# Sixteen packs of memory's keys and values, placed one step of the pairs of heads earlier

## What is computed

```python
def memory_attention(h, mem_n, w_mq, w_mkv, w_mo):
    Bn, S, D = h.shape
    q = (h @ w_mq).reshape(Bn, S, MEM_HEADS, MEM_HEAD_DIM)
    k, v = jnp.split(mem_n @ w_mkv, 2, axis=-1)
...
    s = jnp.einsum('bqhd,bkhd->bhqk', q, k).astype(jnp.float32) * (MEM_HEAD_DIM ** -0.5)
    p = jax.nn.softmax(s, axis=-1)
    o = jnp.einsum('bhqk,bkhd->bqhd', p, v.astype(jnp.float32)).astype(h.dtype).reshape(Bn, S, D)
    return o @ w_mo
```

## Time and profile before

| | us |
|---|---|
| median of 3 runs | 2766.68 (2765.08 to 2767.01) |
| the profiled execution's own time | 2767.14 |
| its span in the trace | 2765.1 |
| PE busy | 2732.9 (99%) |
| DVE busy | 1168.9 (42%) |
| ACT busy | 1033.6 (37%) |
| POOL busy | 1110.3 (40%) |
| mean granted clock | 0.998 |

### The profile page before, as it was taken

How to read it: one execution, slowest core, us unless ns; L and a number is a source line. 1 busy time by engine, 2 the same in 40 slices (tenths; PEclk the granted TensorE clock), 3 DMA queues, 4 the chain that set the end, 5 groups by cost and what they waited for, 6 DMA issues and landing times.

```text
span 2765.1 us, 35465 instructions
## 1 busy us (share of the span) xinstructions
PE 2732.9 (99%) x12412; PEld 2171.7 (79%) x12412; DVE 1168.9 (42%) x1908; ACT 1033.6 (37%) x1584; POOL 1110.3 (40%) x473
## 2 busy tenths in 40 slices
PE   9999999999999999999999999999999999999998
PEld 7777777888888888857888888888888754888887
DVE  5886534655534224256883222122221366422212
ACT  4555534444333223343233222232222466422221
POOL 3234433444444443523224444544445410444443
PEclk9999999999999999999999999999999999999999
DMA  5333322333333332322113323333333210333332
GB/s 168 121 98 116 99 84 63 92 94 103 96 109 97 94 97 93 114 76 88 54 46 107 99 91 106 105 93 99 98 99 107 84 39 10 105 94 101 94 106 84
DMA packets 80029, 257.29 MB, mean 93 GB/s; under 512 B 11576, under 2 KB 16696, under 8 KB 79690
## 3 DMA queue, kind: packets, MB, share of 16 engines
q1 hardware_dynamic: 73712, 245.00, 28.9%
q10 hardware_dynamic: 6234, 11.17, 1.2%
HBM read 249.98 MB, written 6.03 MB: 93 GB/s over the span
## 4 chain that ended last, share of the span: by engine, by line
PE 89%; issue 6%; POOL 2%; DVE 2%; ACT 1%; DMA 0%; POOLq 0%; SPq 0%; DVEq 0%; ACTq 0%
PE ps L813 25%; PE ps L815 25%; PE ps L814 25%; POOL wlo L766 2%; PE ps L1453 1%; PE ps L1435 1%; PE ps L1422 1%; PE ps L1203 1%; PE ps L1232 1%; PE ps L1426 1%; PE ps L1182 1%; PE ps L1109 1%; PE ps L1251 1%; PE ps L1119 1%; PE ps L1042 0%
## 5 line engine op out<-in xcount | busy, mean ns | idle before, releaser
L766 POOL TENSOR_TENSOR wlo<-raw,whi 128x1024 fp32r<-128x1024 f32 x449 | 1098.0, 2449 | 1607.5 <-ACT whi L1522 1582.8
L813 PE MATMUL ps<-lin_hi,whi 128*128 128x512 f32 x2200 | 864.0, 393 | 0.0
L815 PE MATMUL ps<-lin_hi,wlo 128*128 128x512 f32 x2200 | 856.3, 389 | 0.0
L814 PE MATMUL ps<-lin_lo,whi 128*128 128x512 f32 x2200 | 856.1, 389 | 0.0
L1522 ACT ACTIVATE whi<-raw 128x1024 fp32r<-128x1024 f32 x452 | 473.1, 1052 | 524.0 <-PE ps L815 452.1
L813 PEld LDWEIGHTS ps<-lin_hi,whi 128*128 128x128 f32 x2200 | 413.0, 188 | 91.7 <-issue 5.5
L814 PEld LDWEIGHTS ps<-lin_lo,whi 128*128 128x128 f32 x2200 | 413.0, 188 | 88.1 <-issue 3.1
L815 PEld LDWEIGHTS ps<-lin_hi,wlo 128*128 128x128 f32 x2200 | 412.9, 188 | 86.6
L813 PE MATMUL ps<-act_hi,whi 128*128 128x512 f32 x858 | 334.0, 389 | 0.0
L815 PE MATMUL ps<-act_hi,wlo 128*128 128x512 f32 x858 | 333.8, 389 | 0.0
L814 PE MATMUL ps<-act_lo,whi 128*128 128x512 f32 x858 | 333.8, 389 | 0.0
(11 more groups left out here) (406 smaller groups left out, 2762.6 us busy)
## 6 DMA issues: line engine op xcount, KB each, us to landing
raw<-in_packs SPq DMA_DIRECT2D x456, 512.0 KB, 3.6
table<-bias_scratch ACTq DMA_DIRECT2D x12, 256.0 KB, 3.5
bias_scratch<-biasrow ACTq DMA_DIRECT2D x16, 160.0 KB
x<-in_x_t SPq DMA_DIRECT2D x4, 512.0 KB, 8.3
out_t<-x SPq DMA_DIRECT2D x16, 128.0 KB, 1.8
bias_scratch<-biasrow ACTq DMA_DIRECT2D x4, 320.0 KB
mem<-in_mem_t ACTq DMA_DIRECT2D x1, 1024.0 KB, 6.9
pool_count<-in_pool_count ACTq DMA_DIRECT2D x1, 1024.0 KB, 6.2
```

The costliest lines, as they stand in the source:

```text
L766: pool.tensor_tensor(wlo[:, n % 4, :], raw[:, n % 2, :], whi[:, n % 4, :].bitcast(F32), ALU.subtract).then_inc(low_split, 1)
L813: pe.matmul(target, wh, hi[:, k, :], start=(chunk0 + at == 0), stop=False)
L814: pe.matmul(target, wh, lo[:, k, :], start=False, stop=False)
L815: mm = pe.matmul(target, wl, hi[:, k, :], start=False, stop=(chunk0 + at == total - 1))
```

## The change

`KV_FROM` goes from 2 to 1. Memory pack p is now issued in step p + 1 instead of p + 2 on PE, and DVE takes its product out of the bank in step p + 1. Step 1 gets pack 0, ahead of the first transposes; step 16 gets pack 15, and step 17 has no pack. The bound in ACT's loop is written as `LAST_STEP`, which is 18 as `PAIR_STEPS + KV_FROM` was before, so ACT's order stays as it was.

```diff
@@ -113,7 +113,7 @@
 MIXER_A = 16
 PAIR_STEPS = 16
 LAST_STEP = 18
-KV_FROM = 2
+KV_FROM = 1
 
@@ -1819,7 +1819,7 @@
             if s == 0:
                 split_high(N_MIXER + AHEAD)
-            if s < PAIR_STEPS + KV_FROM:
+            if s < LAST_STEP:
                 split_high(N_MIXER + AHEAD + 1 + s)
             between(STEPS_AT + s)
```

## The result

The changed kernel is slower by less than the 0.2% that the prediction takes as what a measurement can tell: median 2769.6 us (2768.04 to 2774.89, 19 runs) against 2765.25 us (2764.93 to 2767.11, 19 runs on the same chip), ratio 1.0018 with an interval of 1.0012 to 1.0024. That is 4.35 us, under the bound of 5.5; the interval lies wholly above 1 and reaches just past the bound. The times of the changed kernel lie in two groups: one at 2768.04 and fourteen from 2769.16 to 2769.95, then four from 2774.5 to 2774.9. The times of before have two as well, fourteen at 2764.9 to 2765.4 and four at 2766.7 to 2767.1, with one at 2765.8 between them. The profile read ahead of the prediction (2767.14) belongs to the upper of them, the one of the changed kernel (2769.16, span 2767.1) to its large group; so between the two profiles there are only 2.0 us.

A forecast was written before the change was run, and what follows sets the result against it. PE, busy 99% of the span, was taken as the bound, with 7.6 us of waits to win. Terms -0.5 + 1.5 + 0 + 2.3 = +3.3 us gave a median of 2770.0 us, range 2765.5 to 2773.0.

The forecast's parts named there:

- Step 1, one long wait in place of two: Start on PE: 4.4 us of waiting ahead of pack 0, step 2's 1.87 us wait gone; gain 0.5 us.
- the step-3 wait of 0.5 us: PE in step 3: expected to wait 0.5 us for DVE's multiplied probabilities, which POOL delays.
- The clock: PE's clock falls to 1.2 GHz in the gap ahead of pack 0, costing 1.5 us (bounds 0 and 3).
- The start as a whole: Steps 1 to 4 on PE: gain of 0.5 us and clock loss of 1.5 us taken together.
- Packs in between: Packs between start and end: weights' low parts there at least 1.5 us in time, so 0 us.
- The end: Steps 16 and 17 and the mixer output's first pack: lost cover costs 1.0 + 1.3 = 2.3 us.
- Waits of step 12: PE's 1.73 us wait in step 12 stays, with the low clock behind it; no change in time.
- A: Rival: clock stays up through the gap ahead of pack 0; +1.8 us, 2768.5 us; chance 0.25.
- B: Rival: step 12's collision of DVE and POOL dissolves, 3.2 us less, 2766.8 us; chance 0.15.
- D: Rival: all 5.0 us of waits in steps 1 to 3 go, end costs nothing; 2761.7 us; chance 0.03.
- C: Rival: low clock for all of pack 0 puts DVE behind two POOL instructions in step 4; 2774.7 us; chance 0.12.

The follow-up runs named there:

- e3: Changed kernel plus twelve unused matmuls of ones in the gap ahead of pack 0; 2770.81 us, ratio 1.0018 to before.
- e2: Kernel before with packs 12 to 15 one step earlier, so step 13 has two packs and step 17 none; 2767.91 us, ratio 1.0009.
- e5: Kernel before with ACT's high part of pack 45 in step 12 behind its two copies of transposed probabilities; 2763.96 us, ratio 0.9994.
- e8: Kernel before with packs 0 to 11 one step earlier, pack 32's high part ahead of step 0's exponentials, late high-part copies in steps 4 and 12; 2762.94 us.
- e4: Changed kernel with ACT's high part of pack 32 ahead of the exponentials of step 0; 2768.07 us, ratio 1.0008 to before.
- e1: Kernel before with packs 0 to 11 one step earlier, none in step 13, packs 12 to 15 as before; 2767.31 us, ratio 1.0008.
- e6: Changed kernel with ACT's high-part copies behind the copies of transposed probabilities in steps 4 and 12; 2767.39 us, ratio 1.0006 to before.
- e7: Kernel before with pack 32's high part ahead of step 0's exponentials and late high-part copies in steps 4 and 12; 2762.4 us, ratio 0.9988.
- e9: Kernel before with pack 32's high part early, late high-part copies in steps 4 and 12, six matmuls of ones ahead of the first transposes; 2762.24 us.

## Why the prediction was right, and where it was off

The forecast of 2770.0 us lies 0.4 over the median and the range holds it; "same" by the bound of 0.2%, with the shift on the predicted side. That it came so near is luck: two errors cancel. It started from 2766.68, the median of three executions, two of which were of the upper group, where nineteen give 2765.25, so 1.4 too high; and it added 3.3 us where the medians differ by 4.35, so 1.05 too little. Between the two profiled executions, which it was worked out for, the difference is 2.0. Its steps did not all hold.

- **Step 1, one long wait in place of two: right.** Pack 0 starts behind 4.38 us for POOL (4.4 predicted), the wait of step 2 is gone. The gain was put at 0.5 us and came out at 1.4 with the clock's 1.5 set apart, or at 1.0 as e3 has it at the full clock (15.57 us for 16.55). The waits up to step 4 fell from 4.99 us to 4.38, by 0.6, as the step-3 wait of 0.5 us that I worked out didn't come. In e3 it is 0.20 us. In the change the slow pack 0 makes PE later (239.33 for 238.10 at the end of pack 2) and DVE hardly (multiplied by 238.98, for 238.57), so the low clock covers it. I had added the two as if they could not overlap: the low clock costs 1.07 us of its 1.5 (16.64 for 15.57). I had also left POOL's times as they were, though its low part of pack 35 starts at 236.02 and not at 233.87, behind ACT's exponentials of step 2. The other 0.8 us is in work that I had not counted: matmuls next to a wait take longer. The transposes of the values last 0.65 us as they stood (the 1.11 us from 225.01 to 226.12, less the 0.46 of waiting) and 0.41 now (231.40 to 231.81); the first transposes 0.46 and 0.31. Packs 0 and 1 take 3.12 and 3.14 us up to the waits behind them before, 0.15 and 0.17 over the 2.97 of a pack with no wait behind it.
- **The clock: right.** It falls in the gap, and pack 0 takes 1.5 us more, as predicted. e3 shows that the gap is the cause. What I had not asked is whether the kernel before always keeps its clock up there: in e2 and e5, with its order, it fell. The start as a whole was predicted at +1.0; it is +0.1 to +0.5 in four profiles of the change. So the start is the part that was mis-sized: by e3, -1.0 and +1.1 in place of -0.5 and +1.5.
- **Packs in between, 0 us: right** (67.37 us before and 67.34 now, from the scores of step 4 to the transposes of step 16).
- **The end, +2.3: right.** It measured +2.2; e2, which has the end alone, lies 2.3 us over before. Its parts were 0.74 and 1.18 us of waiting, for 1.0 and 1.3, and 0.3 in the work next to them.
- **Waits of step 12 "stay, and with it the low clock": right for the profiles, wrong as a statement on the median.** By the profiles that can be priced, the fall costs 1.5 us. All four profiles of the change have it; by the times, the upper group of before (1.5 to 1.9 us over its lower one) is 4 of 19 executions. I had set before and after equal there. That e5, with the meeting gone, has one group only fits this; that the upper group of before is this fall is read from the one profile of it, and not shown for the others. An execution of before without the fall would stand near 2767.14 - 1.5 = 2765.6, and e2's profile without it, less the end's 2.2 us, at 2765.4: both near the lower group. It makes up for the start: 0.1 to 0.5, 2.2 and about 1.5 make 3.8 to 4.2 of the 4.35 us between the medians.
- **Rivals.** A is out in all four profiles; B did not happen. D is out; even e8, where the weights are early and the end is covered, has nothing. C's mechanism is real, but a low clock under pack 0 is not its condition: it came in e3 at the full clock and in e4 at the low one, and stayed away in all four profiles of the change, at the low one. In the change it hangs on how late pack 37 is loaded. The four executions at 2774.5 to 2774.9 lie at C's figure (2774.7), but that is chance, as the figure stands on the base that was 1.4 us too high. They are 5.1 us over the large group, and the meeting of step 4 is worth 1.83 + 1.5 = 3.3 by e3, which leaves 1.8 us without a source. e1 has two of eleven at 2772.4 and 2772.9, and e2 and e6 none; at a rate of 4 in 19, none in eleven would come by chance about once in 13 times. The meeting of step 4 may be part of it, but no profile caught one: their cause stays open.

Two meetings behind one another is what the Trainium skill, "SBUF — State Buffer", section "Who interferes with whom", leads one to expect: VectorE, in the modes that use both ports (`tensor_scalar` can enter them), shares a pair of ports with GpSimd, and whoever issues first holds it for its whole instruction. The rows agree: 4.82 us behind two instructions of POOL, 2.15 where POOL pauses.

## What to carry to other kernels

Before moving work into a wait, ask whether that work's own inputs are there: pack 0's weights were ready only 2.4 us after the wait it was to fill had ended, so the wait only grew. And ask what the moved work covered where it stood: here that was the largest term, 2.2 of 4.35 us. When two engines block each other, shift the trigger of one (e5 to e7, a copy that starts later): it gained 1.8 us and steadied the times, where moving PE's own work gained nothing.

## What the hardware did that I had not expected

- The clock does not follow the length of one wait. It fell behind 1.92 us (e4), 1.93 (e8), 2.00 (e7), 1.97 + 0.39 (e2), 1.98 + 0.28 (e5) and 1.83 (step 4 of e3 and e4), and stayed up in the profile of before through 1.98 + 0.46 and 1.87; behind 1.73 us in step 12 it fell in before and in all four profiles of the change, and not in e1, e2, e3 and e4. The Trainium skill, "TensorE: Matmul & The Clock Gate", section "HAM oscillation — how this bites in real kernels", ties the fall to waits of some microseconds between bursts: the gap of 4.38 us agrees, the shorter ones fell too.
- A lower clock is not always a loss. Under pack 0 it cost e2 nothing, as the next wait shrank, and keeping it up gained nothing in e9 (against e7) and nothing in e3, where the 1.07 us won at the start were lost again in step 4.
- How long the same 512 KB load makes ACT wait differs between executions of one program: 0.32 to 2.46 us for pack 37 in four profiles. Such a difference sets whether two engines meet.
